# Last dense head of a hybrid attention layer: scores in three pairs of PSUM banks, made one step ahead in its first steps

## The reference

```python
def diff_attention(q, k, v, lam, key_ok):
    def attend(q_blk):                       # 128 queries
        s = jnp.einsum('bqhcd,bkhcd->bhcqk', q_blk, k) * scale   # two components c
        s = jnp.where(key_ok, s, NEG)
        p = jax.nn.softmax(s, axis=-1)
        a = p[:, :, 0] - lam * p[:, :, 1]
        return jnp.einsum('bhqk,bkhv->bqhv', a, v)
ob = rms_norm(diff_attention(...), subln_w) * (1 - lam_init)
yb = ob * silu(gb)
```

## Time and profile before

| | |
|---|---|
| median of 3 runs | 1710.3 us (1707.62 to 1711.12) |
| the profiled execution, its time | 1706.29 us |
| its span, first to last instruction | 1705.0 us |
| mean granted clock of TensorE | 0.99 |
| TensorE, VectorE, ScalarE, GpSimd busy | 92%, 63%, 51%, 24% |
| B3 in layer 0, first to last transposes of its tiles | 728.4 to 792.6 us |
| B3 in layer 1, the same | 1544.0 to 1599.9 us |

### The profile page before, as it was taken

One profiled execution on the slowest core, in us unless ns is written; L12 is line 12 of the kernel. 1 busy time (PEld: TensorE's weight loads), 2 busy tenths in 40 slices (PEclk: granted clock), 3 DMA queues, 4 the chain that ended last, 5 costly groups with the idle time before them and its releaser, 6 DMA issues.

```text
span 1705.0 us, 38582 instructions
## 1 busy us (share of the span) xinstructions
PE 1567.1 (92%) x15296; PEld 1463.2 (86%) x15296; DVE 1080.7 (63%) x2461; ACT 875.4 (51%) x2569; POOL 410.1 (24%) x390
## 2 busy tenths in 40 slices
PE   2899999999999989889989999999999899987996
PEld 2899999999888878668989999999999789876896
DVE  6477585446557777775255766844455678787527
ACT  4444545355617676775035445452464477677404
POOL 5333141220121002020453423213103101112044
PEclk9899999999999999999999999999999999999998
DMA  7111201200120111042122102012002111114312
GB/s 264 39 53 37 63 27 32 83 26 14 36 86 17 49 25 49 18 157 99 60 75 83 56 14 64 27 36 78 29 11 71 52 25 50 50 27 146 117 51 100
DMA packets 97859, 102.32 MB, mean 60 GB/s; under 512 B 7504, under 2 KB 87744, under 8 KB 97424
## 3 DMA queue, kind: packets, MB, share of 16 engines
q1 hardware_dynamic: 96720, 98.78, 18.0%
q10 hardware_dynamic: 960, 1.07, 0.2%
HBM read 70.14 MB, written 21.17 MB: 54 GB/s over the span
## 4 chain that ended last, share of the span: by engine, by line
PE 58%; DVE 19%; ACT 11%; POOL 5%; issue 4%; DMA 3%; SPq 0%; ACTq 0%; DVEq 0%; POOLq 0%
PE psum L931 42%; ACT p_b L1601 3%; PE psum L1275 3%; DVE p_b L2137 3%; PE psum L1103 3%; PE psum L1259 3%; POOL w_lo L896 2%; DVE row_max L2123 2%; DVE s_a L1990 2%; PE psum L1000 2%; ACT aT_b L1611 1%; ACT pT_a L1517 1%; POOL w_hi L892 1%; PE psum L978 1%; DMA w_raw<-in_w_in 1%
## 5 line engine op out<-in xcount | busy, mean ns | idle before, releaser
L931 PE MATMUL psum<-w_hi,hT_hi 128*128 128x256 f32 x1824 | 523.6, 287 | 9.4 <-POOL w_lo L896 8.1
L931 PE MATMUL psum<-w_hi,hT_lo 128*128 128x256 f32 x1824 | 513.7, 282 | 0.0
L931 PE MATMUL psum<-w_lo,hT_hi 128*128 128x256 f32 x1824 | 513.5, 282 | 0.0
L892 POOL CAST w_hi<-w_raw 128x512 fp32r<-128x512 f32 (+1 forms) x168 | 112.3, 668 | 1147.8 <-DMA w_raw<-in_w_in 679.6
L931 PEld LDWEIGHTS psum<-w_hi,hT_hi 128*128 128x128 f32 x1824 | 344.2, 189 | 18.5 <-POOL w_lo L896 10.0
L931 PEld LDWEIGHTS psum<-w_hi,hT_lo 128*128 128x128 f32 x1824 | 344.3, 189 | 0.0
L931 PEld LDWEIGHTS psum<-w_lo,hT_hi 128*128 128x128 f32 x1824 | 344.2, 189 | 0.0
L931 PE MATMUL psum<-hT_hi,w_hi 128*128 128x346 f32 (+1 forms) x672 | 226.4, 337 | 9.5 <-DVE hT_lo L1728 9.4
L896 POOL TENSOR_TENSOR w_lo<-w_raw,w_hi 128x512 fp32r<-128x512 f32 (+1 forms) x168 | 215.7, 1284 | 24.1 <-DVE neg_max L2124 12.0
L931 PE MATMUL psum<-hT_hi,w_lo 128*128 128x346 f32 (+1 forms) x672 | 218.1, 325 | 0.0
L931 PE MATMUL psum<-hT_lo,w_hi 128*128 128x346 f32 (+1 forms) x672 | 217.8, 324 | 0.0
(11 more groups left out here) (179 smaller groups left out, 2382.5 us busy)
## 6 DMA issues: line engine op xcount, KB each, us to landing
w_raw<-in_w_in SPq DMA_DIRECT2D x72, 256.0 KB, 3.8
w_raw<-in_w_in SPq DMA_DIRECT2D x28, 512.0 KB, 4.4
h_dram<-hbuf SPq DMA_DIRECT2D x16, 512.0 KB, 2.6
w_raw<-in_w_out SPq DMA_DIRECT2D x16, 512.0 KB, 4.3
hbuf<-h_dram SPq DMA_DIRECT2D x16, 512.0 KB, 6.2
qk_b<-y_dram SPq DMA_DIRECT2D x16, 512.0 KB, 3.3
y_dram<-y_stage SPq DMA_DIRECT2D x96, 64.0 KB, 1.6
qk_t<-rot SPq DMA_DIRECT2D x56, 86.5 KB, 2.2
```

Of the source, the lines that this page charges most:

```text
L892: pool.tensor_copy(hi, raw).then_inc(w_hi_done, 1)
L931: last = nc.tensor.matmul(out_ap, lhs[a](k), rhs[b](k), start=k == 0 and a + b == 0, stop=k == KT - 1 and b == 1)
```

## The change

In B3 alone the scores get three pairs of banks in rotation for tiles 1 to 4: (2,3), (4,5) and (6,7). The scores of tile 1 are issued at the end of B2's last step instead of at the start of B3's first. Those of tile 2 are issued in step 0 after six of the nine values, those of tiles 3 and 4 in steps 1 and 2 between the transposes 0, 1 and the transposes 2. Scores from tile 5 on are issued as before, at the start of the step ahead. On VectorE the first maximum of tiles 2 to 4 moves one step ahead, to before the combination of the tile before; on ScalarE the exponential of component 0 of these tiles moves behind `norm` of the step before its old one, and the exponential of component 1 takes its old place between the copies. `transpose_y` waits in addition until the first exponential of tile 4 has left the banks 6 and 7.

```diff
+LAST = B_HEADS[-1]
+THREE_PAIRS = {(1, 0): 6, (1, 1): 2, (2, 0): 4, (2, 1): 6, (3, 0): 2, (3, 1): 4, (4, 0): 6, (4, 1): 2}
+AHEAD = range(1, 5)
+
+def score_bank(g, t, c):
+    return THREE_PAIRS.get((t, c), 2 + 2 * c) if g == LAST else 2 + 2 * c
+
+def scores_place(l, g, t):
+    out = {"first": [], "turned": [], "half": [], "end": []}
+    after = b_step(l, g, t, 1)
+    if after and not (after[0] == LAST and after[1] in AHEAD):
+        out["first"].append(after)
+    if (g, t) == (B_HEADS[-2], q_tiles(l) - 1):
+        out["end"].append((LAST, 1))
+    if g == LAST and t + 2 in AHEAD:
+        out["half" if t == 0 else "turned"].append((LAST, t + 2))
+    return out
...
# TensorE, pass_b (bank_plan follows the same order)
-                scores(b_step(l, g, t, 1))
+                for step in place["first"]:
+                    scores(step)
                 pe.wait_ge(b_comb, B_STEP[l, g, t])
                 transposes(t, 0)
                 transposes(t, 1)
+                for step in place["turned"]:
+                    scores(step)
...
                 transposes(t, 2)
...
                 values(t, range(6))
+                for step in place["half"]:
+                    scores(step)
                 if not nx and t >= Y_LAG:
+                    wait_read(pe, ("s", l, LAST, AHEAD[-1], 0))
                     transpose_y(l, t - Y_LAG)
                 values(t, range(6, TILES))
...
+                for step in place["end"]:
+                    scores(step)
...
# ScalarE, pass_b
+                first = after and not (g == LAST and after[1] in AHEAD[1:])
                 evac_probs(t, 0)
                 evac_probs(t, 1)
-                if after:
+                if first:
                     exps(after, 0)
+                if not first and after:
+                    exps(after, 1)
                 evac_probs(t, 2)
-                if after:
+                if first:
                     exps(after, 1)
                 values_out(t)
                 norm((g, t))
+                if g == LAST and t + 2 in AHEAD:
+                    exps((g, t + 2), 0)
...
# VectorE, pass_b
+                if after and not (g == LAST and after[1] in AHEAD[1:]):
+                    maximum(after, 0)
                 if after:
-                    maximum(after, 0)
                     maximum(after, 1)
...
                 finish(b_step(l, g, t, -1))
+                if g == LAST and t + 2 in AHEAD:
+                    maximum((g, t + 2), 0)
                 if after:
                     combine(after)
```

More of the change, by code:

```diff
@@ L357, in bank_plan, with scores @@
             for t, parts, _, _ in b_steps(l, nx):
-                if b_step(l, g, t, 1):
-                    for c in range(2):
-                        add(("s", l, *b_step(l, g, t, 1), c), 2 + 2 * c)
+                place = scores_place(l, g, t)
+                def scores(at):
+                    for step in place[at]:
+                        for c in range(2):
+                            add(("s", l, *step, c), score_bank(*step, c))
+                scores("first")
                 if nx and t == n - 1:
@@ L364, in bank_plan @@
                 add(("aT", l, g, t, 1), 1)
+                scores("turned")
                 for h, x, half in parts:
@@ L369, in bank_plan @@
                 add(("o", l, g, t), 1)
+                scores("half")
+                scores("end")
                 if nx and t == n - 2:
```

## The result

The changed kernel takes 1715.44 us (median of 8 runs, 1713.14 to 1719.52) against 1708.9 us for the kernel before on the same chip: a ratio of 1.0037, 95% interval 1.0026 to 1.0048. So it is slower by some 6 us, more than the 0.2% that can be told. The profiled execution took 1718.55 us with a span of 1717.2.

A forecast was written before the change was run, and what follows sets the result against it. It took TensorE, busy 92% of the span, as the bound on average, and B3's early steps as a loop of waits. Lateness of 3.1 us plus clock falls of 5.1 on the 1710.3 median gave 1718.5 us, range 1710.0 to 1722.5.

The forecast's parts named there:

- The walk's sum: B3 in both layers, traced step by step without clock effects: 1.75 + 1.75 - 0.4 = 3.1 us slower.
- Step 0: B3's start, layer 1: VectorE waits for tile 2's scores and takes their maximum before combining tile 1; loss 1.25 us.
- the 0.4 that was counted for the earlier scores of tile 1: Layer 0, front of B3: tile 1's scores could start some 0.6 us sooner; 0.4 us counted as gained.
- Steps 1 to 3: B3, layer 1: a short turn of 5.6 us, then 7.3 and 6.4; scores of tile 5 end 1.75 us late.
- the edits costed at nothing: Extra wait before y transposes, y loads, GpSimd's pieces and subtraction, three banks: no cost beyond the waits already counted.
- ScalarE's queue: B3: tile t+2's exponential waits behind values_out(t), idle by about 1.7 us; tile 3's copies 1.4 us or more after their transposes.
- The clock term: TensorE idle stretches in B3: one fall a layer, 3.4 us, and one in three at four later places, 1.7; together 5.1.
- the 1.83 us wait in front: TensorE's idle wait in the trace of before, after which the clock stayed at 2.4 GHz; read as no harm.
- Case 4: Faster: ScalarE's queue doesn't bind, three turns of 5.1 us, 3.85 us gained a layer, 1702.6 us; chance 0.10.
- The reading of the loop: B3 before: combination, two maxima and exponential make 6.83 us a turn, some 0.5 of it VectorE's wait for GpSimd.
- Case 3: No visible effect: TensorE's lateness at tile 5 is absorbed by slack in the 9.79 us step, 1710.3 us; chance 0.08.

The follow-up runs named there:

- e10: The changed kernel with seven pairs of small filler matmuls in each layer, only where TensorE waits for the combination of tile 1; 1.0026 times the kernel before.
- e8: The changed kernel with 7, 4 and 4 filler matmul calls at TensorE's waits for tile 1's combination, tile 4's scores and tile 3's third transposes; 1.0050 times before.
- e5: The changed kernel with GpSimd's four pieces of the second output chunk beside the maxima of B3's steps 4, 5, 6, 6 instead of 0 to 3; 1.0050 times before.
- e1: The changed kernel with the component 0 exponential of tile t+2 ahead of values_out(t) and the norm on ScalarE, not behind them; 1.0014 times the kernel before.
- e9: The changed kernel run again unaltered, on one chip with other runs; 1.0034 times the kernel before.
- e6: The changed kernel with tile t+2's first exponential ahead of values_out(t) and GpSimd's pieces beside B3's steps 4, 5, 6, 6; 1.0000 times the kernel before.
- e11: The changed kernel with tile t+2's first exponential ahead of values_out(t) and GpSimd's pieces beside B3's steps 0, 3, 4, 5; 0.9997 times the kernel before.
- e7: The kernel before with only GpSimd's four pieces moved to beside B3's steps 4, 5, 6, 6; 1.0011 times the kernel before.
- e12: The kernel before with filler matmuls in B2's last step, between the six and last three values, seven pairs in layer 0, four in layer 1; 0.9987 times before.
- e3: The changed kernel with 14, 10 and 11 filler matmuls at TensorE's waits for tile 1's combination, tile 4's scores and tile 3's third transposes; 1.0051 times before.

## Why the prediction was right, and where it was off

It said 1718.5 us (1710.0 to 1722.5), slower; measured 1715.44. Its difference of 8.2 us compares with 6.5 and 6.8 in two comparisons.

- **The walk's sum, 3.1 us, held, a little too large.** With no fall behind the first turn the scores of tile 5 come at 27.28 in layer 0 (e10), 1.11 later than before, and in layer 1 at 26.85 by the estimate under e8, 1.4 later: 2.5 us. The walk had 1.35 and 1.75, and 27.16 in layer 1.
- **Step 0 held.** VectorE waits for the scores of tile 2 and the turn takes 8.08 (predicted 8.1). In layer 0 it goes from 7.60 to 8.48, 0.88 more where layer 1 has 1.24 more, so the 0.4 that was counted for the earlier scores of tile 1 is there too. In both kernels the fall in B2's last step lengthens this turn.
- **Steps 1 to 3 (the second to fourth turn) held as a sum, not one by one.** Predicted 5.6, 7.3, 6.4, in sum 19.3; e10's layer 0 has 6.59, 6.60, 5.85, in sum 19.04. That the sum is so near is in part luck, since one step of the reading failed and another wait would have taken its place. The step that failed is among the edits costed at nothing: that GpSimd's subtraction "would lose VectorE 0.5 only where it waits anyway". It meets `finish` in the second turn, where VectorE doesn't wait, and costs 0.42 at `coef` and 1.11 at `y_stage`. By e5's layer 0 the turns without it are 5.85, 7.03 and 6.16, near the walk's, and tile 5 comes no sooner (27.18, with it 27.28). The maximum of tile 3 comes later, but ScalarE's queue would have held the next turn by as much.
- **ScalarE's queue was named rightly**, with `values_out` 1.94 and 1.53 late (predicted about 1.7) and the copies of tile 3 1.8 after their transposes. e1 undoes it and wins back 1.0037 - 1.0014, some 4 us.
- **The clock term was near, with luck in the places.** Predicted 5.1 us: a fall behind the first stretch in each layer at 1.7 and a third of one at four more places. Both profiles of the changed kernel (the first and e9) have 6.8 us at the low clock in layer 0 and 3.4 in layer 1, once behind the stretch predicted and once at 1575.2, near the copies of tile 3. Against e10's layer 0 they cost 2.7 and 2.8, against the 26.85 of layer 1 1.5 and 1.7: 4.2 and 4.5 together, so 3.41 us at the low clock cost 1.3 to 1.7. With the 2.5 above the first profile's 4.2 make the 6.7 measured in it; the 26.85 is an estimate, so the split is good to a few tenths. The walk took a fall behind the 2.5 us stretch as certain; over all runs it came in 7 of 14 such stretches (last section), and the 1.83 us wait in front, which it read as harmless from one profile, brought one in 5 of 13.
- **The timed runs on the split.** Every run has its granted clock. Within the kernels of e9's chip a microsecond at 1.2 GHz goes with 0.44 us more time (e9, 12 runs) and 0.38 (before, 35 runs), and e9 spends 46.9 us of a run there, the kernel before 41.0. That makes some 2.4 us of the 6.1 between their means the clock's, by this estimate, and 3.7 the queues'. So the average run falls less often than the profiled ones. Both ways of reckoning agree that neither part is small; the runs don't fix the split closer.
- **Case 4** priced a mended ScalarE at 3 x 1.7 - 1.25 = 3.85 us a layer. e6 and e11 are that case, and it isn't there: the second and third turn are 5.84, held by the wait for scores; the first costs 1.25 and with a fall near it 1.75; the gain of the fourth doesn't reach tile 5. What is left is 0.4 us as measured in layer 1, some 0.9 if no fall came.
- **The reading of the loop** found VectorE's path and called 0.5 us of it a wait for GpSimd. e7 takes that away and the turn loses 0.09. ScalarE's and TensorE's parts of the loop are nearly as long; VectorE's was one bound of several.
- **Case 3** (absorbed by TensorE's slack from tile 4 on) is ruled out: 2.9 us at tile 5 are 2.8 at the end.

## What to carry to other kernels

Before work is moved ahead in one engine's program, write down what it now stands in front of on each of the others: here an exponential made a step early stood behind a wait for TensorE and in front of the copies that TensorE needed, and the gain of the short turns was given back there. Count only turns that reach the point where the next bound begins; e11 had three short turns, which save 3.6 us in layer 1, and 0.4 us arrived. And price the clock as part of a schedule: an idle stretch of TensorE that lies behind a known wait may be worth filling with work that needs nothing, if it ends before the wait does; the gain is at the edge of what the runs can tell here (e10, e12), and fillers that don't end in time cost (e3, 1.0051).

## What the runs showed of the hardware

- **The clock falls after short waits, and not each time.** In the changed kernel it fell to 1.2 GHz behind an idle stretch of 2.52 us in layer 1, and in e9 after two idle waits of 1.16 us each, with short bursts between them:

```profile
1572.65 0.87 PE L1289 MATMUL psum<-ident,p_b 128*128 128x128 f32 x6 [1.16 <-DVE p_b L2181]
1574.69 0.55 PE L1289 MATMUL psum<-ident,p_b 128*128 128x128 f32 x3 [1.16 <-ACT aT_b L1650]
1575.07 2.86 PE L1305 MATMUL psum<-vg_b,aT_b 128*128 128x128 f32 x12
```

  These values take 2.86 us, against 1.60 in the earlier trace rows. Earlier in the same layer of e9 an idle stretch as long as that of the changed kernel was followed by scores at the full clock:

```profile
1559.47 0.88 PE L1289 MATMUL psum<-ident,p_b 128*128 128x128 f32 x6 [2.49 <-DVE p_b L2181]
1560.27 1.66 PE L1133 MATMUL psum<-qk_b 64*128 64x512 f32 x12
```

  Over all kernels that have this stretch (2.48 to 2.52 us ahead of the transposes of tile 1, two layers each), the clock fell around it in 7 of 14. The wait of 2.74 us in B2's last step in layer 0 brought a fall in all 13 kernels that have it, the one of 1.83 us in layer 1 in 5 of 13. So one profile doesn't say whether a wait of this size is harmless. The Trainium skill (TensorE: Matmul & The Clock Gate, "HAM oscillation — how this bites in real kernels") ties a fall to idle gaps longer than either; the traces of this case disagree.
- **Small matmuls hold the clock up at a wait** (e3, e8, e10, e12): where they filled the 2.5 us stretch wholly (e3) or down to some 0.95 (e8, e10), no fall came around it in 6 stretches, against 7 in 14 without them, and in e12's layer 0 none came against 13 in 13. In e12 a run has a mean of 33 us at the low clock instead of 41 (one minus the run's granted clock, times two, times its time), and takes 2.2 us less by the ratio, 3.0 by the medians, some 0.3 to 0.4 us for each. The two places filled account for 3.4 us of the 8 in layer 0 and, when a fall comes there, 3.4 in layer 1; where the rest comes from isn't shown.
- **VectorE waits for GpSimd.** `y_stage`, 0.35 us alone, took 1.46 beside GpSimd's 1.28 us subtraction; `coef` 0.57 instead of 0.15 beside a cast of 0.64. The Trainium skill (SBUF — State Buffer, "Terms") says that VectorE and GpSimd share a port pair which is locked for a whole instruction; by that rule the one that comes second waits until the other's instruction has ended. These rows agree: `coef` ends with the cast at 1563.25 and `y_stage` at 1564.76, 0.15 after the subtraction's 1564.61. The maxima, which read PSUM, keep their 1.22 us beside the same work.
- **Identical code varies by more than the change.** Between the combination of tile 7 in layer 0 and that of tile 0 in layer 1 all kernels run the same instructions (but for e12's four filler calls in layer 1), and the profiled executions take from 762.3 us (before) to 768.3 (e8). The shortest two (before, e12) have 6.8 us at the low clock in it, those from 765.6 up 10.2 to 13.7; but at 13.7 they still range from 765.6 to 768.3, which the clock doesn't explain. One profile's span can't judge a change of this size; the delay measured inside the stretch that was changed can.
